# Experts phase: GpSimd's row gathers written out one by one, read from the lists in place

## What is computed

```python
eidx = jnp.take_along_axis(comb_idx, fi, axis=-1)
w = jax.nn.softmax(fv, axis=-1)
act = jax.nn.gelu(jnp.einsum("thkd,td->thk", u[eidx], tb).astype(jnp.float32))
return jnp.einsum("thk,thkd->td", (w * act).astype(tb.dtype), v[eidx])
```

## Time and profile before

| what | value |
|---|---|
| time, median of 3 runs | 4871.53 us (4870.77 to 4876.87) |
| the profiled execution | 4885.86 us, of which the span 4883.7 us |
| POOL busy over the span | 1518.7 us (31%) |
| DVE, PE busy over the span | 3520.8 us (72%), 4508.2 us (92%) |
| gathers in the profile (L2289, L2291) | 512 and 512, mean 1114 and 1249 ns |
| copies (L2283) | 128, mean 752 ns |
| DMA busy in the slices of the experts phase | 9 tenths or more |

### The profile page before, as it was taken

How to read it: one execution, slowest core, us unless ns; L and a number is a source line. 1 busy time by engine, 2 the same in 40 slices (tenths; PEclk the granted TensorE clock), 3 DMA queues, 4 the chain that set the end, 5 groups by cost and what they waited for, 6 DMA issues and landing times. The chain is left out here.

```text
span 4883.7 us, 82658 instructions
## 1 busy us (share of the span) xinstructions
PE 4508.2 (92%) x28695; PEld 4184.8 (86%) x28695; DVE 3520.8 (72%) x6718; ACT 1813.4 (37%) x3800; POOL 1518.7 (31%) x1358
## 2 busy tenths in 40 slices
PE   7999999799989899969885769999999999999996
PEld 5999999799975598968774669999999999999995
DVE  3101555466754333447999979999999999999998
ACT  3111333244435431234444963333333333333332
POOL 0000000011110000000000017777777777777773
PEclk9999999899988899979997999999999999999998
DMA  4332222344433244338995569999999999999996
GB/s 164 107 139 97 82 91 87 124 141 140 146 110 58 63 166 184 135 116 306 345 330 197 206 240 364 361 372 371 371 376 372 374 362 371 370 372 377 377 370 248
DMA packets 351143, 1170.28 MB, mean 240 GB/s; under 512 B 40160, under 2 KB 91808, under 8 KB 344608
## 3 DMA queue, kind: packets, MB, share of 16 engines
q0 software_dynamic: 147456, 536.94, 29.2%
q1 hardware_dynamic: 160544, 483.06, 27.7%
q10 hardware_dynamic: 43008, 148.53, 8.1%
HBM read 971.20 MB, written 197.46 MB: 239 GB/s over the span
## 5 line engine op out<-in xcount | busy, mean ns | idle before, releaser
L2291 POOL DMA_INDIRECT ex_vr<-in_expert_v,ex_at x512 | 639.5, 1249 | 236.7 <-issue 150.3
L2289 POOL DMA_INDIRECT ex_ur<-scr_u_rows,ex_at x512 | 570.1, 1114 | 278.2 <-issue 118.1
L2478 DVE SCALAR_TENSOR_TENSOR ex_acc_rows<-ex_vr,ex_wt,ex_acc_rows 128x1024 f32<-128x1024 f32 x512 | 648.9, 1277 | 1.1 <-ACT ex_wt L2394 0.2
L2470 DVE SCALAR_TENSOR_TENSOR ex_ur<-ex_ur,h_rows 128x1024 f32<-128x1024 f32 x512 | 615.9, 1217 | 33.5 <-DMA ex_ur<-scr_u_rows,ex_at 32.6
L2283 POOL COPY ex_at<-picked_at 128x4 uint32 x128 | 96.3, 752 | 1469.0 <-POOLq L125 1468.5
L990 POOL TENSOR_TENSOR sd_cts<-sd_cT,sd_ea 128x512 f32<-128x512 f32 x72 | 98.5, 1368 | 1262.4 <-ACT sd_ea L880 1262.4
L2301 PE MATMUL ex_ps<-hd_hi,ex_u_hi 128*128 128x320 f32 x2048 | 470.4, 311 | 20.9 <-PEq L125 16.4
L2301 PE MATMUL ex_ps<-hd_lo,ex_u_hi 128*128 128x320 f32 x2048 | 470.0, 311 | 0.0
L2301 PE MATMUL ex_ps<-hd_hi,ex_u_lo 128*128 128x320 f32 x2048 | 469.1, 310 | 0.0
L2392 ACT ACTIVATE ex_gel<-ex_dot 128x1 f32<-128x1 f32 x512 | 103.6, 202 | 897.8 <-DVE ex_ur L2470 897.8
L479 DVE TENSOR_TENSOR pr_w_lo<-pr_w,pr_w_hi 128x1024 fp32r<-128x1024 f32 x56 | 68.6, 1226 | 489.4 <-ACT pr_w_hi L475 489.4
(11 more groups left out here) (365 smaller groups left out, 11142.9 us busy)
## 6 DMA issues: line engine op xcount, KB each, us to landing
pk_raw_u<-in_expert_u SPq DMA_DIRECT2D x128, 512.0 KB, 6.5
scr_u_rows<-pk_rows_u ACTq DMA_DIRECT2D x128, 512.0 KB, 6.2
ex_u<-in_expert_u SPq DMA_DIRECT2D x128, 512.0 KB, 6.8
ex_v<-in_expert_v SPq DMA_DIRECT2D x128, 512.0 KB, 8.4
scr_gate<-gt_stage SPq DMA_DIRECT2D x10, 4096.0 KB, 12.6
ex_gate<-scr_gate SPq DMA_DIRECT2D x32, 1280.0 KB, 8.7
pr_w<-in_w_main SPq DMA_DIRECT2D x58, 512.0 KB, 4.6
scr_xbc<-pr_out ACTq DMA_DIRECT2D x32, 576.0 KB, 3.8
```

What stands on the lines that cost most here:

```text
L2289: nc.gpsimd.indirect_dma_start(out=ur[:, s], out_offset=None, in_=scr["u_rows"], in_offset=by).then_inc(ur_in[s], 16)
L2291: nc.gpsimd.indirect_dma_start(out=vr[:, s], out_offset=None, in_=io["expert_v"].rearrange("j i d -> (j i) d"), in_offset=by).then_inc(vr_ ...
L2470: v.scalar_tensor_tensor(out=ur[:, s], in0=ur[:, s], scalar=1.0, in1=rows[:, s], op0=ALU.mult, op1=ALU.mult, accum_out=dot[:, m:m + 1]).th ...
L2478: v.scalar_tensor_tensor(out=acc_g[:, s], in0=vr[:, s], scalar=wt[:, m:m + 1], in1=acc_g[:, s], op0=ALU.mult, op1=ALU.add).then_inc(row_r[ ...
```

## The change

In the experts phase POOL's loop becomes straight code: 1024 gathers, each with one wait against a constant, which is part of the gather's own instruction. A gather takes its 128 row numbers from column `n` of `picked_at` where it lies. The copies, the waits before and after them, the increments of `cleared` and all register work are gone, with the tiles `ex_at` and `ex_share` and two semaphores. ACT takes the share from `picked_share` at an address from a register. Which buffer each gather waits for, and the order of the gathers, stay.

```diff
-            at_now, share_now = sb2("ex_at", [P, 2, ST], U32), sb2("ex_share", [P, 2, ST])
...
-            now_r, gel_r, wt_r, cleared = sem("ex_nowr"), sem("ex_gelr"), sem("ex_wtr"), sem("ex_cleared")
+            gel_r, wt_r = sem("ex_gelr"), sem("ex_wtr")
...
-                def free(sem_, value):
-
-                    pool.wait_ge(sem_, value)
-                    pool.sem_inc(cleared, 1)
-
-                with pool.Fori(0, BATCHES) as b:
-                    for h in range(2):
-                        for s in range(ST):
-                            pool.wait_ge(row_r[s], b * 2 + h + START)
-                        nc.gpsimd.tensor_copy(at_now[:, h], at[:, :, ds(b * 2 + h, 1)].rearrange("p s j -> p (s j)")).then_inc(now_r, 1)
-                        nc.gpsimd.tensor_copy(share_now[:, h], share[:, :, ds(b * 2 + h, 1)].rearrange("p s j -> p (s j)")).then_inc(now_r, 1)
-                        free(now_r, b * 4 + (h + 1) * 2 + START)
-                        for s in range(ST):
-                            by = bass.IndirectOffsetOnAxis(ap=at_now[:, h, s:s + 1], axis=0)
-                            free(dot_r[s], b * 2 + h + START)
-                            nc.gpsimd.indirect_dma_start(out=ur[:, s], out_offset=None, in_=scr["u_rows"], in_offset=by).then_inc(ur_in[s], 16)
-                            free(row_r[s], b * 2 + h + 2 * START)
-                            nc.gpsimd.indirect_dma_start(out=vr[:, s], out_offset=None, in_=io["expert_v"].rearrange("j i d -> (j i) d"), in_offset=by).then_inc(vr_in[s], 16)
+                for n in range(2 * BATCHES):
+                    for s in range(ST):
+                        by = bass.IndirectOffsetOnAxis(ap=at[:, s, n:n + 1], axis=0)
+                        pool.wait_ge(dot_r[s], n + START)
+                        nc.gpsimd.indirect_dma_start(out=ur[:, s], out_offset=None, in_=scr["u_rows"], in_offset=by).then_inc(ur_in[s], 16)
+                        pool.wait_ge(row_r[s], n + 2 * START)
+                        nc.gpsimd.indirect_dma_start(out=vr[:, s], out_offset=None, in_=io["expert_v"].rearrange("j i d -> (j i) d"), in_offset=by).then_inc(vr_in[s], 16)
...
-                    nc.scalar.activation(wt[:, m:m + 1], gel[:, m:m + 1], ACT.Copy, scale=share_now[:, m // ST, m % ST:m % ST + 1]).then_inc(wt_r, 1)
+                    nc.scalar.activation(wt[:, m:m + 1], gel[:, m:m + 1], ACT.Copy, scale=share[:, m % ST, ds(b * 2 + m // ST, 1)]).then_inc(wt_r, 1)
```

## The result

The changed kernel takes 4841.4 us (median of 8 runs, 4836.9 to 4860.7) beside 4874.2 us for the kernel before (8 runs, 4867.1 to 4879.4). Its profiled execution took 4842.3 us, with a span of 4840.3.

The account below looks back on a forecast made before the run. DVE, PE and DMA engines were nearly full, and DVE's 33.6 us of waiting was the reach. Long gathers 8.2 + start 1.3 + small waits 3 = 12.5 us off the 4871.5 median: 4859 us, range 4848 to 4876.

Parts of the forecast that it names:

- the pauses: POOL's sequencer stands still up to 3 us in seven batches, 16.2 us over; mostly put to profiling, nothing counted.
- more: Rival: pauses are in every execution and each costs 1 to 2 us less after the change; 4849 us, chance 0.12.
- DVE's run of four: Four DVE operations with two SBUF operands each, from 4028.09; the last `v` gather would start at about 4027.9.
- The small waits: DVE waits of 0.1 to 0.4 us, mostly in batches loading gates; earlier second-half gathers win 3 us, 0 to 6.
- Long gathers: Fourteen 4.9 us gathers, mostly a batch's last `v` gather or its neighbour, would go: 8.2 us won, 0 to 9.6.
- The single gathers: Signs: second half's first gather 2.5 us earlier, first half's last `u` gather still 1.97 us, shortest batches still 29.45.
- The batch of 29.44 us: Shortest batch before, with all four copies in it; taken as showing that copies do not hold up DVE.
- the text's own condition: The forecast is wrong if gathers freed by a wait start more than 0.3 us behind it; 0.05 to 0.25 expected.
- no change: Rival: gathers start 0.3 us or more after release, long gathers and small waits stay; 4870 us, chance 0.30.
- The start: The phase's first gather no longer waits for two copies and two increments: 1.3 us won, 0 to 1.4.
- ACT and code: ACT's register instruction has 0.5 us of cover; fetching POOL's 1024 instructions costs 0 to 3 us; both counted as 0.
- the prediction's four fetches: Trainium skill: code is refilled in blocks of 256 instructions, so POOL's 1024 would be four fetches and cost nothing.

Follow-up runs that it names:

- the repeat: The changed kernel, unaltered, profiled and timed a second time against the kernel before: ratio 0.9938.
- The 16 delays: Two copies and a wait added 16 times, to the changed kernel (ratio to before 0.9945) and to before with only its loop written out (1.0075).

## Why the prediction fell short

**The step that failed is the pauses.** It put the profiled execution's 14.3 us over the median down to them and counted none of their cost. Two profiles of before agree to 0.3 us in the batches, and two of after likewise; their difference, 30.5 us, is close to the timed 32.8 and to 30.7 in the repeat. So the pauses' cost is in every profile and, by that agreement, in the timed runs too, which have no trace of their own. The 14 us then lay ahead of the phase for the most part, where one kernel's two profiles differ by 5.7 to 8 us and all runs reach from 2875 to 2895 us. The text also said that pauses come 200 us apart whatever POOL does; they stand at fixed gathers, which is some 200 us here.

Their cost goes not because they go. The worst stands at gather 113. The same stretch of after, POOL and then DVE:

```profile
3098.14 1.19 POOL L2278 DMA_INDIRECT ex_ur<-scr_u_rows,picked_at  x1 [0.30 <-issue]
3100.27 1.35 POOL L2280 DMA_INDIRECT ex_vr<-in_expert_v,picked_at  x1 [0.94 <-issue]
...
3107.43 0.94 POOL L2278 DMA_INDIRECT ex_ur<-scr_u_rows,picked_at  x1 [0.30 <-issue]
...
3118.98 1.21 DVE L2459 SCALAR_TENSOR_TENSOR ex_ur<-ex_ur,h_rows 128x1024 f32<-128x1024 f32 x1
```

POOL idles 0.94 us instead of 2.19 there. The last `u` gather of the half starts at 3107.43, 1.6 us ahead of the next batch; before it started at 3126.43, 2.3 us behind the opening at 3124.09. What that costs stands in SyncE's rows of before, and POOL's beside them:

```profile
3126.26 0.33 SPq L2233 DMA_DIRECT2D ex_gate<-scr_gate  x1
3126.78 0.90 SPq L2237 DMA_DIRECT2D ex_v<-in_expert_v  x2
```

```profile
3126.43 1.56 POOL L2289 DMA_INDIRECT ex_ur<-scr_u_rows,ex_at  x1 [0.30 <-issue]
```

2.3 MB of gates and weights went out 0.2 us ahead of it and just behind. The gather's rows landed 10.3 us after its end (9.4 in the second profile of before), against 6.8 in after, and DVE waited 4.17 us. So a pause of 2 us became a batch 5.6 us too long. In after this pause is shorter as well as better covered. Three remain at full length, 2.06 to 2.14 us at gathers 325, 537 and 855. The batches behind them were 1.75, 3.56 and 0.74 us too long before; they are 0.05, 0.27 and 0.04 now, and DVE waits 0.2 us in all. There the pause stayed and its cost went. The rival called *more* had this mechanism and gave 4849; it was short because it took each pause as 1 to 2 us of POOL's time and left out what being late costs in the queues. The 16 delays show the same with a known dose. That a late gather can also run into DVE's run of four is what the kernel before with fewer weight bytes shows.

**The small waits** (3 us forecast, of 9.2) were undersized too: with the pauses' 16.2 and the long gathers' 8.2 gone, 6.1 of the 30.5 us remain for them. The reason is the same. The sum moved each gather's issue and left its way to landing alone. The gather that matters most is one that the sum did not move at all, the last `u` gather of the first half, for which DVE asks 24 us into the batch. Its start did not change, yet it lands 5.2 us after its end instead of 6.2 (medians over the batches), and in the batches that load gates 5.1 instead of 7.1. There it came just as DVE asked for it, 0.02 us ahead, and now has 1.8 us to spare. Copies ahead of the even rounds alone bring both back, 8.1 us and 0.02. The last `u` gather of the second half lands 8.0 us after its end before and 6.5 after; in the kernel before with fewer weight bytes it is 5.7, which fits that it shared the engines with the weight loads. Its slack on DVE grew from 1.3 to 4.1 us, of which 1.3 was foreseen and 1.5 is the shorter landing. The weight loads gained as well, as the DMA view of 3000 to 4700 us shows (issues, KB, median us to landing; before, then after):

```profile
ex_v<-in_expert_v SPq DMA_DIRECT2D x114, 512.0 KB, 9.9
```

```profile
ex_v<-in_expert_v SPq DMA_DIRECT2D x114, 512.0 KB, 7.5
```

The second profiles have 9.9 and 8.3 us here.

**Long gathers** (8.2 us): that they go held, 14 became 1, and putting back the copies of the even rounds brought 15 back. The price did not hold as a price of their own. The twelve batches that had one before and no pause were 8.2 us over, and those 8.2 us are gone; but with the copies of the even rounds alone 15 long gathers cost 0.02 to 0.15 us each. A long gather costs 0.7 us only where the gathers behind it have no spare time, so the number came out right partly by luck. It was close, too. The gather starts at 4023.42, 0.05 us ahead of the run, not the 0.2 that was worked out.

**The single gathers:** the first gather of the second half is 2.45 us earlier (2.5 said); the last of the first half still takes 1.97 us; no batch is shorter than before. The Trainium skill has copies that read SBUF hold up two-input DVE operations ("SBUF — State Buffer", section "Who interferes with whom"); by it batches would have become shorter, and they are not. The batch of 29.44 us that the prediction held against this could not show it, as every batch of before has its four copies; the profile after can. A gather freed by a `dots` starts 0.34 us behind it (3998.88 to 3999.22) instead of 0.9. That is outside the 0.05 to 0.25 expected and by the text's own condition a sign for *no change*; it did not decide, because that gather is still held by the DVE operation beside it and ends when it did, and the last gather had 0.05 us left.

**The start** gave 0.2 us instead of 1.3: from its first instruction of the phase, DVE reached the first batch in 22.2 us instead of 22.3 (22.2 and 22.9 in the second profiles). It took 22.1 us too with copies and increments kept and only the loop written out. Perhaps the landings waited for crowd with SyncE's first loads of gates and weights, which POOL's earlier issue does not move; this was not tried.

**ACT and code** cost nothing that shows, as said; the one wait of 0.2 us for `ex_wt`, in the last batch, was there before. The weight starts 0.33 us after its gelu instead of 0.24 and still ends 0.4 us ahead of its reader:

```profile
3998.99 0.20 ACT L2381 ACTIVATE ex_gel<-ex_dot 128x1 f32<-128x1 f32 x1 [2.23 <-DVE ex_ur L2459]
3999.32 0.29 ACT L2383 ACTIVATE ex_wt<-ex_gel,picked_share 128x1 f32<-128x1 f32 x1
```

Fetches of code rose by 8 packets (57 to 65) and 0.06 MB, in bytes what the prediction's four fetches hold.

## What to carry to other kernels

An engine that is 74% busy can still have no spare time: look at how long it waits for the others. POOL waited for DVE 144 us of 1800 before and 356 after, 2.4 and 5.8 us a batch, and a delay of 2.5 us was absorbed in the changed kernel and cost 1.8 us in one with the old copies and increments. Where several small savings lie on one chain, cost them together and against its disturbances, since the first half of them may bring little and the rest much. And a transfer issued late costs more than its lateness when bulk loads go out in between: price the landing, not the issue. Before a cost is put down to the profiler, see whether it stands at the same place in every profile, and where in the program the surplus of the profiled execution really lies. And a row that is seen beside a wait, as the long gathers here, has not been priced until it is seen without it.

## What the runs showed that was not expected

POOL's sequencer pauses 106 gathers apart, or a multiple, at the same gathers in both profiles of each kernel; how long it stands at one of them can differ (0.98 and 2.54 us at gather 749 of before). The pause's idle time at gather 325 is 3.7 us with increments, 2.5 in the kernel before, 2.1 without either, 0.9 with copies and no increments. What stands between gathers is not all of it: with the share read in place it is 3.8 there, and at gather 537 the kernel before has 2.1, with fewer weight bytes 3.8. Three awaited gathers ahead of the loop don't shift it, three between rounds shift it by 18.

Four increments and waits in a row delayed the next gather at four of 16 places, by 0.5 to 0.8 us, although a single wait with its increment, put ahead of a gather that DVE frees, costs 0.54 (0.88 us behind the `dots` before, 0.34 after). And code that no edit touches takes up to 20 us more or less ahead of the phase from one profile to the next, more than most single edits in this kernel bring. The sum of the batches repeats better: four profiles of the changed kernel with the same or nearly the same code lie from 1857.5 to 1859.2 us, three of the kernel before from 1885.7 to 1889.3.
